# Opening of a two-layer decoder trunk: first conditioning vectors summed by the vector engine from smaller loads, the second in a PSUM bank of its own, unread products between one-column products

## The chip, the cores and the metric

The kernel runs on one core of a Trainium2 chip. The time is device microseconds of one execution of the whole program; several runs give a median. One further execution is profiled, and all rows below come from it.

## The reference

Two layers. Each layer has a mixer (latent attention with 4 heads beside a gated short convolution) and a channel mixer (dense SwiGLU in layer 0, top-2 of 8 SwiGLU experts in layer 1). x has 256 tokens of 1024 values. All of it is conditioned by six vectors of 1024 values per layer:

```
c_act = jax.nn.silu(c)
for l in range(DEPTH):
    mod = (c_act @ w_ada[l] + b_ada[l])[:, None, :]
    shift1, scale1, gate1, shift2, scale2, gate2 = jnp.split(mod, 6, axis=-1)
    h = x * (1 + scale1) + shift1
    y = hybrid_mixer(h, ...)                  # begins with z = h @ w_in
    x = layer_norm(DEEPNORM_ALPHA * x + gate1 * y, ln1_g[l], ln1_b[l])
    h = x * (1 + scale2) + shift2
    ...
```

w_ada is 1024 x 6144 per layer, so each vector costs 4 MB of weights and a product with a single row. Nothing in the kernel can begin before shift1 and scale1 of layer 0.

## The kernel before

All weights come through a ring of 7 slots of 2 MB (`raw`), filled by SyncE (SP) in the order of the list `loads`; before it fills a slot again, SP waits for a semaphore that says that the slot's old content is used. The list begins with four strips of w_ada (half a vector's weights each: strips 0 and 1 make vector 0, the shift; strips 2 and 3 vector 1, the scale), then x, then `wa`, `wb`, `wc` (parts of w_in), then further strips between the parts of the mixer's weights. Strips below `EARLY` come in two halves, with a semaphore for each.

A vector is formed so. A strip lies in its slot as four chunks of 128 rows and 1024 columns. The vector engine (DVE, `ada_part`, L950) multiplies a chunk by a column of c_act and adds it to `ada_acc`, whose start value the scalar engine (ACT, `ada_init`, L559) writes from the bias. TensorE (PE) then sums `ada_acc` over its 128 rows by eight one-column products against `ones` (L1543), which also turn the vector into 8 columns. For strips 1, 2 and 3 (`PE_ROWS`) PE takes the last chunk itself, by eight one-column products with c_act (L1539). Both vectors go through PSUM bank 7; the list `BANK7` gives the order of its uses, with the transpose of the small parameters (L1580) between the two, and ACT empties the bank after each (`drain_ada`, L570).

PE runs its own queue in order. Ahead of the products of each of the two vectors stand products of 512 columns that go to bank 4 and that nobody reads (L1576, L1583): they keep PE at work. After the second vector PE transposes x (L1570, 16 transposes); ACT and DVE write h_t from it (L587, L968); and L1607 multiplies h_t by wa, 16 products of 448 columns in 12 us. Behind it come the units of the mixer (L1590 to L1592), each a third of a product in split precision. A product of fp32 operands leaves two records in the trace, a transpose one.

Of the kernel before, what the change touches and what calls it, by code (L numbers as in the profile page):

```python
# [79 lines left out]
BANK7 = [("ada", 0, 0, 0), "params", ("ada", 0, 1, 0)]  # L80
PE_ROWS = (1, 2, 3)
# [8 lines left out]
EARLY = 4  # L90
# [27 lines left out]
def trunk(nc, a, out):  # L118
    with ExitStack() as ctx:
# [5 lines left out]
        def sem(name):  # L125
# [155 lines left out]
        half_full = [sem(f"half_full{k}") for k in range(EARLY)]  # L281
# [4 lines left out]
        prm_loaded, x_loaded, ln_loaded, rt_loaded = (sem("prm_loaded"), sem("x_loaded"), sem("ln_loaded"),  # L286
                                                      sem("rt_loaded"))
# [53 lines left out]
        def load_ada(l, n):  # L341
            k = ADA_ORDER.index(("ada", l, n))
            src, parts = strip_src(l, n), 2 if k < EARLY else 1
            loads.append((("ada", l, n), [(q * SLOT // parts, (q + 1) * SLOT // parts, 4 // parts,
                                           src[:, q * 4 // parts:(q + 1) * 4 // parts, :]) for q in range(parts)],
                          (bank7_full, BANK7.index(("ada", l, n // 2, 0)) + 1) if k < EARLY else (ada_summed, k + 1)))

# [5 lines left out]
        for l in range(L):  # L353
            z0 = ZA
            load_pe(("wa", l), [(0, KC * ZA, KC, win_src(l, 0, ZA))], (za_mm, TT * (l + 1)))
# [34 lines left out]
        for n, (name, parts, _) in enumerate(loads):  # L390
            filled[n % RING] += 16 * (1 if n < EARLY else len(parts))
            place_of[name] = n % RING
            full_at[name] = filled[n % RING]
        L0 = len(loads)

# [54 lines left out]
        def _(sp):  # L450
            sp.dma_start(c_col[:, :], a["c"].rearrange("a (k p) -> p (a k)", p=P),
                         allow_slow_non_contiguous=True).then_inc(c_loaded, 16)
            for n, (name, parts, _) in enumerate(loads):
                if n >= RING:
                    s, value = loads[n - RING][2]
                    sp.wait_ge(s, value)
                for lo, hi, chunks, src in parts:
                    dst = raw[n % RING][:, lo:hi].rearrange("p (c n) -> p c n", c=chunks)
                    sp.dma_start(dst, src).then_inc(half_full[n] if n < EARLY and lo == 0 else slot_full[n % RING], 16)
                if name == ("ada", 0, 3):  # L460
                    for t in range(TT):
                        sp.dma_start(x_sb[:, t, :], a["x"][0, t * P:(t + 1) * P, :]).then_inc(x_loaded, 16)
# [82 lines left out]
        def _(act):  # L545
# [30 lines left out]
            def modulate(v, l, row, last, t):  # L576

                if v == 0:
                    act.wait_ge(bank7_free, bank7(last) + 1)
# [37 lines left out]
            act.wait_ge(consts, 1)  # L617
            drain_ada(0, 0)
            act.wait_ge(bank7_full, bank7("params") + 1)
            act.activation(prm[:, :], ps[:, 7, 0:PRM], ACT.Copy).then_inc(bank7_free, 1)  # L620
            drain_ada(0, 1)

            def mixer(l):
                if l == 0:
                    modulate(0, 0, 0, ("ada", 0, 1, 0), 0)
                    modulate(0, 0, 0, ("ada", 0, 1, 0), 1)
# [28 lines left out]
                unit(2)  # L655
                for t in range(TT):
# [265 lines left out]
        def _(dve):  # L922
# [8 lines left out]
            def ada_part(l, n, first, last):  # L931
# [4 lines left out]
                for c in range(first, last):  # L936
                    if c == 0:
                        if k < EARLY:
                            dve.wait_ge(half_full[k], 16)
                        else:  # L940
                            wait_load(dve, name)
                        if kh == 0:
                            dve.wait_ge(ada_set, k // 2 + 1)
                        else:
                            dve.wait_ge(ada_summed, k)
                    if c == 2 and k < EARLY:
                        wait_load(dve, name)
                    if c == 3 and k in PE_ROWS:
# [10 lines left out]
            def modulate(v, l, row, last, t):  # L959
                if v == 0:  # L960
                    dve.wait_ge(bank7_free, bank7(last) + 1)
# [38 lines left out]
            dve.wait_ge(consts, 1)  # L1000
            dve.wait_ge(c_ready, 1)
            for n in range(4):
                ada(0, n)

# [41 lines left out]
            def mixer(l, behind):  # L1046
                if l == 0:
                    modulate(0, 0, 0, ("ada", 0, 1, 0), 0)
                    modulate(0, 0, 0, ("ada", 0, 1, 0), 1)
# [152 lines left out]
            dve.wait_ge(x_loaded, 16 * TT)  # L1202
# [318 lines left out]
        def _(pe):  # L1521
# [4 lines left out]

            def ada(l, vec, part=0):
# [4 lines left out]
                if 2 * k < EARLY:  # L1532
                    pe.wait_ge(c_ready, 1)
                    rows = [n for n in (2 * vec, 2 * vec + 1) if n in PE_ROWS]
                    for n in rows:
                        wait_load(pe, ("ada", l, n))
                        w = slot_of(("ada", l, n))[:, 3 * D:4 * D]
                        for c in range(KC):
                            pe.matmul(ps[:, 7, c:c + 1], w[:, c * P:(c + 1) * P], c_act[:, 4 * (n % 2) + 3:4 * (n % 2) + 4],  # L1539
                                      start=(n == rows[0] and c == 0), stop=False, skip_group_check=True)  # L1540
                    pe.wait_ge(ada_summed, 2 * (k + 1))
                    for c in range(KC):
                        m = pe.matmul(ps[:, 7, c:c + 1], acc[:, c * P:(c + 1) * P], ones[:, 0:1],  # L1543
                                      start=False, stop=True, skip_group_check=True)
                    m.then_inc(bank7_full, 1)
                    return
# [14 lines left out]
            def turn_input(v, t):  # L1561
# [4 lines left out]
                else:  # L1566
                    pe.wait_ge(x_loaded, 16 * TT)
# [26 lines left out]
            def mixer(l):  # L1594
# [4 lines left out]
                wait_load(pe, ("wa", l))  # L1599
                wa = slot_of(("wa", l))[:, 0:KC * ZA].rearrange("p (c n) -> p c n", c=KC)  # L1600
                order = ((0, 4, 1, 5, 2, 6, 3, 7), range(KC))[l]
                for t in range(TT):
                    for n, c in enumerate(order):
# [403 lines left out]
```

## Time and profile before

| | |
|---|---|
| three runs | 1488.74, 1495.96, 1496.12 us; median 1495.96 |
| profiled execution, its own time | 1490.59 us |
| its span, first to last instruction | 1488.8 us |
| mean granted TensorE clock | 0.984 of 2.4 GHz |
| PE busy | 1430.2 us, 96% |
| DVE busy | 1262.4 us, 85% |
| ACT busy | 1000.1 us, 67% |

Times in rows are counted from the start of the span. A busy PE is not PE at its peak: its work is pipelined, and the ends of its records are modelled, so what a product costs is read from start to start. The granted clock is printed as a part of 2.4 GHz; its two levels are 1.00 and 0.50.

### The profile page before, as it was taken

What the parts mean: (1) busy time and instruction counts of PE and PEld (TensorE: products, weight loads), DVE (VectorE), ACT (ScalarE), POOL (GpSimd) and SP (SyncE); (2) the same over time, 40 slices, a digit from 0 to 9 for tenths busy, and PEclk for the clock granted to TensorE, in tenths of its full rate; (3) what the DMA queues carried; (4) which work ended last, traced back from release to release, by engine and by line L of the source; (5) the groups of instructions that cost most, each with busy time, mean ns of one, the idle gap of its engine ahead of it and who ended that gap; (6) DMA issues with size and microseconds to landing.
All of it is one profiled execution on the core that took longest, in us unless ns stands there. A gap on an engine that the chain in (4) does not pass through costs nothing.

```text
span 1488.8 us, 20198 instructions
## 1 busy us (share of the span) xinstructions
PE 1430.2 (96%) x7131; PEld 1169.6 (79%) x7131; DVE 1262.4 (85%) x1432; ACT 1000.1 (67%) x1188; POOL 19.8 (1%) x60
## 2 busy tenths in 40 slices
PE   7999999999999999999999999999999999999994
PEld 5875899996955788788788878878878877887883
DVE  5796887776768898898898989889889889889997
ACT  2523444354333788888888888888888888887883
POOL 1000000000000000000000000000000000001000
PEclk8999999999998999999999999999999999999998
DMA  9993678876572599999999999999999999999960
GB/s 363 395 403 143 224 289 326 298 269 253 215 297 89 217 390 356 364 386 355 368 372 365 365 362 391 359 362 375 362 367 372 361 368 371 374 358 378 410 252 30
DMA packets 203457, 482.18 MB, mean 324 GB/s; under 512 B 6928, under 2 KB 31614, under 8 KB 203402
## 3 DMA queue, kind: packets, MB, share of 16 engines
q1 hardware_dynamic: 198832, 470.31, 84.2%
q0 software_dynamic: 1584, 5.77, 1.0%
q10 hardware_dynamic: 2986, 5.38, 1.0%
q8 instruction: 33, 0.54, 0.1%
q14 instruction: 22, 0.18, 0.0%
HBM read 475.67 MB, written 5.77 MB: 323 GB/s over the span
## 4 chain that ended last, share of the span: by engine, by line
PE 84%; DVE 7%; ACT 6%; issue 3%; DMA 1%; ACTq 0%; DVEq 0%; SPq 0%
PE ps L1590 24%; PE ps L1592 23%; PE ps L1591 23%; ACT w_hi L809 2%; PE ps L1751 2%; PE ps L1928 2%; DVE low L1257 2%; PE ps L1607 2%; DVE ada_acc L950 1%; ACT h_t L840 1%; PE ps L1708 1%; PE ps L1552 1%; DMA raw<-in_w_ada_dram 1%; PE ps L1570 1%; ACT L809 1%
## 5 line engine op out<-in xcount | busy, mean ns | idle before, releaser
L1257 DVE TENSOR_TENSOR low<-raw,w_hi 128x1024 fp32r<-128x1024 f32 x672 | 790.3, 1220 | 67.7 <-ACT w_hi L809 53.1
L809 ACT ACTIVATE w_hi<-raw 128x1024 fp32r<-128x1024 f32 x672 | 701.3, 1062 | 132.2 <-PE ps L1592 127.8
L1590 PE MATMUL ps<-w_hi,h_lo 128*128 128x512 f32 x896 | 356.6, 398 | 10.3 <-DVE low L1257 9.8
L1592 PE MATMUL ps<-w_hi,h_hi 128*128 128x512 f32 x896 | 349.8, 390 | 0.0
L1591 PE MATMUL ps<-low,h_hi 128*128 128x512 f32 x896 | 349.1, 390 | 0.0
L1590 PE MATMUL ps<-w_hi,hid_lo 128*128 128x512 f32 x536 | 211.4, 394 | 7.4 <-DVE low L1257 4.9
L1590 PEld LDWEIGHTS ps<-w_hi,h_lo 128*128 128x128 f32 x896 | 168.2, 188 | 54.0 <-DVE low L1257 19.7
L1591 PE MATMUL ps<-low,hid_hi 128*128 128x512 f32 x536 | 208.8, 390 | 0.0
L1592 PE MATMUL ps<-w_hi,hid_hi 128*128 128x512 f32 x536 | 208.8, 390 | 0.0
L1592 PEld LDWEIGHTS ps<-w_hi,h_hi 128*128 128x128 f32 x896 | 168.2, 188 | 36.3
L1591 PEld LDWEIGHTS ps<-low,h_hi 128*128 128x128 f32 x896 | 168.5, 188 | 33.1
L950 DVE SCALAR_TENSOR_TENSOR ada_acc<-raw,c_act,ada_acc 128x1024 f32<-128x1024 f32 x93 | 119.0, 1281 | 11.2 <-ACT ada_acc L559 8.3
L1590 PEld LDWEIGHTS ps<-w_hi,hid_lo 128*128 128x128 f32 x536 | 100.7, 188 | 33.5 <-DVE low L1257 8.2
L1592 PEld LDWEIGHTS ps<-w_hi,hid_hi 128*128 128x128 f32 x536 | 100.6, 188 | 21.2
L1591 PEld LDWEIGHTS ps<-low,hid_hi 128*128 128x128 f32 x536 | 100.7, 188 | 19.8
L1590 PE MATMUL ps<-h_hi,low 128*128 128x256 f32 x320 | 92.6, 289 | 1.0 <-ACT sil L746 1.0
L1591 PE MATMUL ps<-h_lo,w_hi 128*128 128x256 f32 x320 | 90.5, 283 | 0.0
L1592 PE MATMUL ps<-h_hi,w_hi 128*128 128x256 f32 x320 | 90.5, 283 | 0.0
L1186 DVE TENSOR_TENSOR low<-raw,w_hi 128x1024 fp32r<-128x1024 f32 x62 | 74.9, 1222 | 13.5 <-ACT w_hi L760 12.6
L1192 DVE TENSOR_TENSOR h_t<-ps,sil 128x512 f32<-128x512 f32 x67 | 46.2, 690 | 42.1 <-ACT sil L746 24.2
L760 ACT ACTIVATE w_hi<-raw 128x1024 fp32r<-128x1024 f32 x62 | 63.6, 1053 | 26.3 <-PE ps L1592 25.9
L1590 PEld LDWEIGHTS ps<-h_hi,low 128*128 128x128 f32 x320 | 61.3, 191 | 2.5 <-ACT sil L746 1.2
(335 smaller groups left out, 1423.2 us busy)
## 6 DMA issues: line engine op xcount, KB each, us to landing
raw<-in_moe_w_gate_dram SPq DMA_DIRECT2D x56, 2048.0 KB, 9.3
raw<-in_moe_w_up_dram SPq DMA_DIRECT2D x56, 2048.0 KB, 9.6
raw<-in_moe_w_down_dram SPq DMA_DIRECT2D x56, 2048.0 KB, 9.2
raw<-in_w_ada_dram SPq DMA_DIRECT2D x20, 2048.0 KB, 9.0
raw<-in_w_in_dram SPq DMA_DIRECT2D x6, 2048.0 KB, 16.0
raw<-in_ffn_w_gate_dram SPq DMA_DIRECT2D x11, 1024.0 KB, 8.2
raw<-in_ffn_w_up_dram SPq DMA_DIRECT2D x11, 1024.0 KB, 10.5
raw<-in_ffn_w_down_dram SPq DMA_DIRECT2D x11, 1024.0 KB, 9.5
```

The source lines that it names most:

```text
L760: act.activation(w_hi[:, u % SRING, :], slot_of(name)[:, lo:lo + UNIT], ACT.Copy).then_inc(unit_hi, 1)
L809: act.activation(w_hi[:, (FF_UNITS + k) % SRING, :], raw[moe_slot(m)][:, (k % 4) * UNIT:(k % 4 + 1) * UNIT], ACT.Copy).then_inc(unit_hi, 1)
L950: ins = dve.scalar_tensor_tensor(acc, w[:, c, :], c_act[:, 4 * kh + c:4 * kh + c + 1], acc, ALU.mult, ALU.add)
L1186: dve.tensor_tensor(low_of(name)[:, lo:lo + UNIT], slot_of(name)[:, lo:lo + UNIT], w_hi[:, u % SRING, :].bitcast(F32), ALU.subtract).then_ ...
L1192: dve.tensor_tensor(hid, ps[:, 1, :].rearrange("p (f n) -> p f n", f=4), sil[:, :].rearrange("p (f n) -> p f n", f=4), ALU.mult).then_inc( ...
L1257: dve.tensor_tensor(low[moe_slot(m)][:, part], raw[moe_slot(m)][:, part], w_hi[:, q, :].bitcast(F32), ALU.subtract).then_inc(unit_lo, 1)
L1590: pe.matmul(o, x_lo, hi, start=first, stop=False, skip_group_check=True)
L1591: pe.matmul(o, x_hi, lo, start=False, stop=False, skip_group_check=True)
L1592: return pe.matmul(o, x_hi, hi, start=False, stop=last, skip_group_check=True)
L1607: m = pe.matmul(ps[:, 4 + t, 0:ZA], h_t[:, c, t * P:(t + 1) * P], wa[:, c, :], start=(n == 0), stop=(n == KC - 1))
L1751: m = pe.matmul(ps[:, (0, 5)[t] + half, :], a_t[:, c, t * P:(t + 1) * P], oa[:, c, half * 512:(half + 1) * 512], start=(c == 0), stop=(c = ...
L1928: m = pe.transpose(ps[:, 2, f * P:(f + 1) * P], hid[:, f, :], ident[:, :])
```

## The change

- Strips 0 to 3 come in 4, 2, 2 and 4 parts (`EARLY_PARTS`), and wa of layer 0 in two.
- DVE takes all chunks of strips 0, 1 and 3; of strip 2 PE takes two (`PE_CHUNKS`) and DVE two. The first chunk of a vector is a plain multiplication into `ada_acc`, with no start value; the last chunk of strip 3 is added in two halves.
- The bias of both vectors comes from PE: 16 one-column products of the 12 bias rows with a column of the identity (`early_bias`). Vector 1 is summed in bank 6, with semaphores `scale_full` and `scale_ready`.
- Ahead of the first sum stand 12 unread products of 512 columns instead of 5; the 3 ahead of the second vector are gone, and one stands behind each pair of one-column products with strip 2, 8 in all.
- The transpose of the parameters and their copy, and the start value of vector 3, move behind the transposes of x and behind ACT's first three `w_mix`.
- PE and DVE wait for the two halves of x apart, and L1607 takes the chunks in the order 0 to 7 (before: 0, 4, 1, 5, 2, 6, 3, 7).

```
-BANK7 = [("ada", 0, 0, 0), "params", ("ada", 0, 1, 0)]
-PE_ROWS = (1, 2, 3)
+BANK7 = [("ada", 0, 0, 0), "params"]
-EARLY = 4
+EARLY_PARTS = (4, 2, 2, 4)
+EARLY = len(EARLY_PARTS)
+PE_CHUNKS = (2, 3)
...
             def ada_init(k):
 
-                if k >= 2:
+                if k == 3:
+                    act.wait_ge(scale_full, 1)
+                elif k >= 2:
...
+            def drain_scale():
+                act.wait_ge(scale_full, 1)
+                act.activation(modc[:, 0, 1, :], ps[:, 6, 0:KC], ACT.Identity, bias=ones[:, 0:1]).then_inc(scale_ready, 1)
...
-            act.wait_ge(ident_ready, 1)
-            act.wait_ge(bias_loaded, 16)
-            ada_init(0)
-            ada_init(1)
...
+            act.wait_ge(bias_loaded, 16)
             drain_ada(0, 0)
-            act.wait_ge(bank7_full, bank7("params") + 1)
-            act.activation(prm[:, :], ps[:, 7, 0:PRM], ACT.Copy).then_inc(bank7_free, 1)
-            drain_ada(0, 1)
+            drain_scale()
...
                 unit(2)
+                if l == 0:
+                    act.wait_ge(bank7_full, bank7("params") + 1)
+                    act.activation(prm[:, :], ps[:, 7, 0:PRM], ACT.Copy).then_inc(bank7_free, 1)
+                    ada_init(3)
...
+                    if k == 2 and c in PE_CHUNKS:
                         continue
-                    ins = dve.scalar_tensor_tensor(acc, w[:, c, :], c_act[:, 4 * kh + c:4 * kh + c + 1], acc, ALU.mult, ALU.add)
-                    if c < (2 if k in PE_ROWS else 3):
+                    col = c_act[:, 4 * kh + c:4 * kh + c + 1]
+                    if k < EARLY and kh == 0 and c == 0:
+                        link(dve.tensor_scalar(acc, w[:, c, :], col, None, ALU.mult))
+                        continue
+                    if k == EARLY - 1 and c == 3:
+                        dve.scalar_tensor_tensor(acc[:, 0:512], w[:, c, 0:512], col, acc[:, 0:512], ALU.mult, ALU.add).then_inc(ada_half, 1)
+                        dve.scalar_tensor_tensor(acc[:, 512:], w[:, c, 512:], col, acc[:, 512:], ALU.mult, ALU.add).then_inc(ada_summed, 1)
+                        continue
...
+            def early_bias(k, bank):
+
+                for c in range(KC):
+                    pe.matmul(ps[:, bank, c:c + 1], ada_bias[0:L * VECS, c * P:(c + 1) * P], ident[0:L * VECS, k:k + 1],
+                              start=(c == 0), stop=False, skip_group_check=True)
+
+            def early_sum(k, bank, chunks):
+
+                for c in chunks:
+                    m = pe.matmul(ps[:, bank, c:c + 1], ada_acc[:, k, c * P:(c + 1) * P], ones[:, 0:1],
+                                  start=False, stop=True, skip_group_check=True)
+                return m
+
+            def warm_load(n, times):
+
+                wait_load(pe, ("ada", 0, n))
+                for _ in range(times):
+                    pe.matmul(ps[:, 4, :], ident[:, :], slot_of(("ada", 0, n))[:, 0:512], start=True, stop=True)
...
             pe.wait_ge(ident_ready, 1)
-            wait_load(pe, ("ada", 0, 0))
-            for _ in range(5):
-                pe.matmul(ps[:, 4, :], ident[:, :], slot_of(("ada", 0, 0))[:, 0:512], start=True, stop=True)
-            ada(0, 0)
+            pe.wait_ge(bias_loaded, 16)
+            early_bias(0, 7)
+            early_bias(1, 6)
+            warm_load(0, 12)
+            pe.wait_ge(ada_summed, 2)
+            early_sum(0, 7, range(KC)).then_inc(bank7_full, 1)
+            wait_load(pe, ("ada", 0, 2))
+            w = slot_of(("ada", 0, 2)).rearrange("p (c n) -> p c n", c=4)
+            for c in range(KC):
+                for q in PE_CHUNKS:
+                    pe.matmul(ps[:, 6, c:c + 1], w[:, q, c * P:(c + 1) * P], c_act[:, q:q + 1],
+                              start=False, stop=False, skip_group_check=True)
+                pe.matmul(ps[:, 4, :], ident[:, :], w[:, 0, 0:512], start=True, stop=True)
+            pe.wait_ge(ada_half, 1)
+            early_sum(1, 6, range(KC // 2))
+            pe.wait_ge(ada_summed, 4)
+            early_sum(1, 6, range(KC // 2, KC)).then_inc(scale_full, 1)
+            turn_input(0, 0)
+            turn_input(0, 1)
             use_bank7("params")
             pe.wait_ge(prm_loaded, 16 * PRM_LOADS)
             pe.transpose(ps[:, 7, 0:PRM], prm_rows[:, :], ident[0:PRM, 0:PRM]).then_inc(bank7_full, 1)
-            wait_load(pe, ("ada", 0, 2))
-            for _ in range(3):
-                pe.matmul(ps[:, 4, :], ident[:, :], slot_of(("ada", 0, 2))[:, 0:512], start=True, stop=True)
-            ada(0, 1)
-            turn_input(0, 0)
-            turn_input(0, 1)
```

Two places show how the instructions move. The first is PE from its first product to the products with wa; an arrow points from the operands to the output, `raw` is a slot, `x16` counts products that are alike. Before:

```order
L1576 MATMUL ps<-raw,ident 128x512 x5
L1539 MATMUL ps<-c_act,raw 128x1 x8
L1543 MATMUL ps<-ones,ada_acc 128x1 x8
L1580 MATMUL ps<-ident,prm_rows 128x110
L1583 MATMUL ps<-raw,ident 128x512 x3
L1539 MATMUL ps<-c_act,raw 128x1 x16
L1543 MATMUL ps<-ones,ada_acc 128x1 x8
L1570 MATMUL ps<-ident,x_sb 128x128 x16
L1607 MATMUL ps<-raw,h_t 128x448 x16
```

The same stretch of PE in the changed kernel; of the eight pairs with their unread product the first two stand here:

```order
L1558 MATMUL ps<-ident,ada_bias 128x1 x16
L1572 MATMUL ps<-raw,ident 128x512 x12
L1564 MATMUL ps<-ones,ada_acc 128x1 x8
L1616 MATMUL ps<-c_act,raw 128x1 x2
L1618 MATMUL ps<-raw,ident 128x512
L1616 MATMUL ps<-c_act,raw 128x1 x2
L1618 MATMUL ps<-raw,ident 128x512
...
L1564 MATMUL ps<-ones,ada_acc 128x1 x8
L1602 MATMUL ps<-ident,x_sb 128x128 x16
L1627 MATMUL ps<-ident,prm_rows 128x110
L1652 MATMUL ps<-raw,h_t 128x448 x16
```

Ahead of the products with wa stood 8 unread and 40 one-column products; now there are 20 and 48, and the transpose of the parameters has moved behind those of x.

The second place is ACT from the first activation to the squares of the mixer (`gb_t,ssq`). Before, without the ten small loads between:

```order
L607 ACTIVATE c_act<-c_col 128x8
L559 ACTIVATE ada_acc<-ada_bias,ident 128x1024 x2
...
L570 ACTIVATE modc<-ps,eps 128x8
L559 ACTIVATE ada_acc<-ada_bias,ident 128x1024
L620 ACTIVATE prm<-ps 128x110
L570 ACTIVATE modc<-ps,ones 128x8
L559 ACTIVATE ada_acc<-ada_bias,ident 128x1024
L587 ACTIVATE h_t<-ps,modc 128x128 x8
...
L639 ACTIVATE w_mix<-raw 128x1024
L658 ACTIVATE gb_t,ssq<-ps 128x256
```

The same stretch of ACT in the changed kernel:

```order
L624 ACTIVATE c_act<-c_col 128x8
...
L587 ACTIVATE modc<-ps,eps 128x8
L572 ACTIVATE ada_acc<-ada_bias,ident 128x1024
L576 ACTIVATE modc<-ps,ones 128x8
L604 ACTIVATE h_t<-ps,modc 128x128 x8
...
L651 ACTIVATE w_mix<-raw 128x1024
L670 ACTIVATE prm<-ps 128x110
L572 ACTIVATE ada_acc<-ada_bias,ident 128x1024
L674 ACTIVATE gb_t,ssq<-ps 128x256
```

The start values of vectors 0 and 1 are gone; the copy of prm and the start value of vector 3 have moved from ahead of h_t to ahead of the squares.

## Rows read from the trace of the kernel before

**Rows 1.** The page, part 4: the chain that ended last, by engine.

```profile
PE 84%; DVE 7%; ACT 6%; issue 3%; DMA 1%; ACTq 0%; DVEq 0%; SPq 0%
```

**Rows 2.** Timeline of PE, 0 to 48 us: start, us, engine, line, operation, records, idle before.

```profile
10.31 6.86 PE L1576 MATMUL ps<-raw,ident 128*128 128x512 f32 x10 [10.31 <-DMA raw<-in_w_ada_dram]
17.01 1.84 PE L1539 MATMUL ps<-c_act,raw 128*128 128x1 f32 x16
18.71 1.93 PE L1543 MATMUL ps<-ones,ada_acc 128*128 128x1 f32 x16
21.20 4.45 PE L1583 MATMUL ps<-raw,ident 128*128 128x512 f32 x6
25.49 3.93 PE L1539 MATMUL ps<-c_act,raw 128*128 128x1 f32 x32
29.29 3.55 PE L1543 MATMUL ps<-ones,ada_acc 128*128 128x1 f32 x16
32.70 3.29 PE L1570 MATMUL ps<-ident,x_sb 128*128 128x128 f32 x16
35.83 12.19 PE L1607 MATMUL ps<-raw,h_t 128*128 128x448 f32 x32
```

**Rows 3.** Timeline of DVE, two pieces of its sums.

```profile
9.21 13.11 DVE L950 SCALAR_TENSOR_TENSOR ada_acc<-raw,c_act,ada_acc 128x1024 f32<-128x1024 f32 x10 [8.25 <-ACT ada_acc L559]
...
26.31 1.28 DVE L950 SCALAR_TENSOR_TENSOR ada_acc<-raw,c_act,ada_acc 128x1024 f32<-128x1024 f32 x1 [0.22 <-DMA raw<-in_w_ada_dram]
```

**Rows 4.** PE by stretches: length, busy (records), granted clock, DMA share, GB/s.

```profile
10.30:15.00 4.70, 4.69 (x6) 1.00 1.02 394
15.00:17.00 2.00, 2.00 (x5) 1.00 1.05 413
21.90:25.20 3.30, 3.30 (x5) 0.50 1.05 409
25.30:28.60 3.30, 3.30 (x30) 1.00 1.02 409
28.70:35.40 6.70, 6.70 (x33) 0.50 1.05 404
35.60:40.00 4.40, 4.40 (x16) 1.00 1.05 409
```

**Rows 5.** The chain in order of time, a run of transposes at the upper level.

```profile
144.91 0.87 PE ps L1570 x8
```

**Rows 6.** Timeline of SP's queue, issues behind x: start, time to issue.

```profile
14.28 10.73 SPq L459 DMA_DIRECT2D raw<-in_w_in_dram  x2
29.68 5.69 SPq L459 DMA_DIRECT2D raw<-in_w_ada_dram  x1
```

**Rows 7.** Timeline of ACT.

```profile
7.92 1.15 ACT L559 ACTIVATE ada_acc<-ada_bias,ident 128x1024 f32<-128x1024 f32 x1 [3.35 <-DMA ada_bias<-in_b_ada_dram]
...
32.88 0.27 ACT L570 ACTIVATE modc<-ps,ones 128x8 f32<-128x8 f32 x1 [10.69 <-PE ps L1543]
...
48.06 0.38 ACT L658 ACTIVATE gb_t<-ps 128x256 f32<-128x256 f32 x1 [4.53 <-PE ps L1607]
```

**Rows 8.** Groups of DVE by form: busy us, mean ns, idle before.

```profile
L996 DVE TENSOR_SCALAR yv<-yv,meanvar,rstd 128x1024 f32<-128x1024 f32 x6 | 4.9, 812 | 0.2
```

**Rows 9.** DMA issues up to 75 us: size, median us from issue to landing.

```profile
raw<-in_w_in_dram SPq DMA_DIRECT2D x1, 1792.0 KB, 19.5
```

**Rows 10.** Groups of weight loads by form.

```profile
L1539 PEld LDWEIGHTS ps<-c_act,raw 128*128 128x128 f32 x48 | 6.1, 203 | 1.3 <-issue 1.3
...
L1853 PEld LDWEIGHTS ps<-router_b,ones 1*128 1x128 f32 x4 | 0.6, 182 | 0.0
```

**Rows 11.** All engines by stretches; the last two numbers are DMA share and GB/s.

```profile
50.00:75.00 25.00, 25.00 (x212) 25.00 (x211) 19.45 (x27) 11.76 (x17) 0.00 (x0) 1.00 0.97 385
...
100.00:110.00 10.00, 10.00 (x46) 7.18 (x46) 9.72 (x14) 2.60 (x3) 0.00 (x0) 0.98 1.06 404
```

**Rows 12.** Waits from 35 us to the end that a DMA ended: total us, times, longest.

```profile
ACT w_mix L639 <- DMA raw<-in_w_in_dram: 0.6, 1, 0.6
```

More of the change, by code:

```diff
@@ L280, in trunk @@
         slot_full = [sem(f"slot_full{k}") for k in range(RING)]
-        half_full = [sem(f"half_full{k}") for k in range(EARLY)]
+        part_full = [[sem(f"part_full{k}_{q}") for q in range(parts - 1)] for k, parts in enumerate(EARLY_PARTS)]
+        wa_half, ada_half = sem("wa_half"), sem("ada_half")
+        scale_full, scale_ready = sem("scale_full"), sem("scale_ready")
         ada_set, ada_summed = sem("ada_set"), sem("ada_summed")
@@ L354, in trunk @@
             z0 = ZA
-            load_pe(("wa", l), [(0, KC * ZA, KC, win_src(l, 0, ZA))], (za_mm, TT * (l + 1)))
+            halves = 2 if l == 0 else 1
+            load_pe(("wa", l), [(q * KC * ZA // halves, (q + 1) * KC * ZA // halves, KC // halves,
+                                 win_src(l, 0, ZA)[:, q * KC // halves:(q + 1) * KC // halves, :]) for q in range(halves)],
+                    (za_mm, TT * (l + 1)))
             load_pe(("wb", l), [(0, SLOT, KC, win_src(l, z0, z0 + D_CONV))], (mix_used, MIX_UNITS * l + 4))
@@ L390, in trunk @@
         for n, (name, parts, _) in enumerate(loads):
-            filled[n % RING] += 16 * (1 if n < EARLY else len(parts))
+            filled[n % RING] += 16 * (1 if n < EARLY or name == ("wa", 0) else len(parts))
             place_of[name] = n % RING
@@ L394, in trunk, with part_sem @@
         L0 = len(loads)
+        def part_sem(n, name, q, parts):
+            if q < parts - 1 and n < EARLY:
+                return part_full[n][q]
+            return wa_half if name == ("wa", 0) and q == 0 else slot_full[n % RING]
         def slot_of(name):
@@ L456, in _ @@
                     sp.wait_ge(s, value)
-                for lo, hi, chunks, src in parts:
+                for q, (lo, hi, chunks, src) in enumerate(parts):
                     dst = raw[n % RING][:, lo:hi].rearrange("p (c n) -> p c n", c=chunks)
-                    sp.dma_start(dst, src).then_inc(half_full[n] if n < EARLY and lo == 0 else slot_full[n % RING], 16)
+                    sp.dma_start(dst, src).then_inc(part_sem(n, name, q, len(parts)), 16)
                 if name == ("ada", 0, 3):
                     for t in range(TT):
-                        sp.dma_start(x_sb[:, t, :], a["x"][0, t * P:(t + 1) * P, :]).then_inc(x_loaded, 16)
+                        sp.dma_start(x_sb[:, t, :], a["x"][0, t * P:(t + 1) * P, :]).then_inc(x_loaded[t], 16)
             def expert_loads(i, e, first, store):
@@ L937, in ada_part @@
                     if c == 0:
[L938 to L939 removed]
+                        if k >= EARLY:
+                            wait_load(dve, name)
+                        if kh == 1:
+                            dve.wait_ge(ada_summed, k)
+                        elif k >= EARLY:
+                            dve.wait_ge(ada_set, k // 2 - 1)
+                    if k < EARLY and c % (4 // EARLY_PARTS[k]) == 0:
+                        q = c * EARLY_PARTS[k] // 4
+                        if q < EARLY_PARTS[k] - 1:
+                            dve.wait_ge(part_full[k][q], 16)
                         else:
                             wait_load(dve, name)
[L942 to L948, printed above, removed]
[L949 to L951 removed]
+                    if k == 2 and c in PE_CHUNKS:
+                        continue
+                    col = c_act[:, 4 * kh + c:4 * kh + c + 1]
[6 more added lines that the diff above has]
+                        continue
+                    ins = dve.scalar_tensor_tensor(acc, w[:, c, :], col, acc, ALU.mult, ALU.add)
+                    if c < (min(PE_CHUNKS) - 1 if k == 2 else 3):
                         link(ins)
@@ L1200, in hidden_lo @@
                                   ALU.subtract).then_inc(hid_lo_ready, 1)
-            dve.wait_ge(x_loaded, 16 * TT)
+            for t in range(TT):
+                dve.wait_ge(x_loaded[t], 16)
             mixer(0, lambda t: None)
@@ L1531, in ada @@
                 acc = ada_acc[:, k % 2, :]
[L1532 to L1546, printed above, removed]
                 pe.wait_ge(ada_summed, 2 * (k + 1))
@@ L1597, in mixer @@
                     turn_input(2, 0)
-                wait_load(pe, ("wa", l))
+                if l == 0:
+                    pe.wait_ge(wa_half, 16)
+                else:
+                    wait_load(pe, ("wa", l))
                 wa = slot_of(("wa", l))[:, 0:KC * ZA].rearrange("p (c n) -> p c n", c=KC)
-                order = ((0, 4, 1, 5, 2, 6, 3, 7), range(KC))[l]
                 for t in range(TT):
-                    for n, c in enumerate(order):
+                    for n, c in enumerate(range(KC)):
+                        if l == 0 and t == 0 and n == KC // 2:
+                            wait_load(pe, ("wa", l))
                         if l == 1 and t == 0 and n == 6:
```

25 lines of the change are left out of this document (13 added, 12 removed).

## The prediction

> **What bounds the kernel now.** I read the page first. PE is busy for 96% of the span, and the chain that ended last is 84% PE [rows 1], so time in the opening counts only where PE is what is waited for. Then I took the timeline of PE up to its first large product, L1607 [rows 2]. The reader is to see one idle stretch, up to 10.31 us, when the first strip of w_ada is there, and behind it work almost without a gap until L1607 starts at 35.83. That work is 8 products of 512 columns that nobody reads (16 records, since one fp32 product leaves two), 40 one-column products (80 records: 16, 16, 32 and 16) and 17 transposes. So PE's own queue bounds the opening, not the vector engine and not the loads: DVE's last product of the second vector starts at 26.31 and takes 1.28 [rows 3], it is over at 27.6, and PE comes to the sum that reads it only at 29.29 [rows 2]. Last I took the granted clock by stretches [rows 4]: 0.50 (1.2 GHz) from 21.9 to 25.2 and from 28.7 to 35.4, 1.00 (2.4 GHz) between. Both falls come behind stretches in which PE ran little but one-column products. At the very start the column says 1.00, but there 6 records lie in 4.70 us and right after 5 in 2.00, so the first 4.7 us of work ran at the lower level too.
>
> **Prices.** A 512-column record costs 0.43 us at the upper level and 0.85 at the lower (10 records from 10.31 to 17.01: 4.7/0.85 + 2.0/0.43 = 10.2). A one-column record costs 0.106 to 0.12 at the upper level (16 in 1.70, 32 in 3.80, start to start), I take 0.115, and 0.213 at the lower (16 from 29.29 to 32.70) [rows 2, 4]. A transpose at the upper level is 0.87/8 = 0.109 [rows 5]; the 16 of the opening took 3.13, at the lower.
>
> **Loads.** The same bytes come in the same order. The diff adds five issues on SP's queue (4+2+2+4 in place of 8 for w_ada, 2 in place of 1 for wa); they lie beside transfers that hold SP anyway (5.69 us for one issue at 29.68 [rows 6]). The last part of strip 3 therefore lands at 26.3 as now. The smaller first parts let DVE start near 6 us in place of 9.21, where it waits for ACT's start value [rows 3, 7], but then it follows the loads: its end is 26.3 plus two halves of 0.67, 27.6, the same as now. I cost this at nothing. The first product as tensor_scalar, 0.81 us by the nearest row [rows 8] against 1.28, twice, lies ahead of a wait for a load: nothing too. wa in halves saves nothing: the whole of it lands at 14.28 + 19.5 = 33.8 [rows 6, 9], before L1607 starts.
>
> **PE, step by step.** PE's queue is in order, so each item delays all behind it.
> 1. Bias products: 16 of one column, 32 records, as soon as ada_bias is there, 7.92 by ACT's row [rows 7]. PE is cold, so 32 x 0.213 = 6.8 us, to 14.75. The bounds are 32 x 0.115 = 3.7 and 6.8; I take the upper, because the first products of the kernel now run at the lower level and no rise has come behind one-column products [rows 2, 4]. That they have 12 rows changes little: the load of a weight of one row takes 182 ns, of 128 rows 203 in the mean of both levels [rows 10].
> 2. Unread products: 12, so 24 records, 24 x 0.427 = 10.25 at the upper level, plus half of the time spent at the lower. That time is now 4.7 us at the start and 3.4 from 21.8; I take 3.6 (bounds 2.5 and 4.7): 12.1, to 26.85. Strip 0 is there at 10.3 and DVE's first vector at about 18.4 (7 products from 9.21 now), so neither ends this step.
> 3. The sum of the first vector, 16 records: 1.85, to 28.7. ACT's drain behind it is not late for anything; it also frees slots 0 and 1, to which SP comes at 29.68 [rows 6].
> 4. The third strip: eight times two one-column products and one of 512 columns, 8 x (4 x 0.115 + 2 x 0.427) = 10.5, to 39.2.
> 5. The sum of the second vector, which DVE has had ready since 27.6: 1.85, to 41.05.
> 6. 16 transposes: 1.75 at the upper level, to 42.8, and the one of the parameters, 0.1. ACT writes the scale in 0.27 [rows 7] and its first h_t beside them.
>
> L1607 starts at 42.9 in place of 35.83: **+7.0 us**. The same by difference: 12 more unread products, +10.25; eight more one-column products, +1.8; an earlier start, -2.25; idle gaps gone, -0.5; less time at the lower level, -2.3.
>
> What else moves has cover. The copy of prm (some 0.3) and the start value of vector 3 (1.15) now stand on ACT behind w_mix, ahead of the squares of L658; ACT waits 4.53 us for PE there [rows 7], and without that cover they would cost 1.4. SP waits for scale_full at 41.05, where it waited for bank 7 until 32.8; queued behind are strips and wu. It has issued 19.7 MB by then (four strips, x, wa, wb, wc, two strips) and about 15.5 have moved at 0.41 MB/us [rows 11], so the DMA engines have work for 10 us more.
>
> **Does it pass on?** From 35 us to the end the waits name a DMA as releaser once, for 0.6 us (ACT, for wb) [rows 12], where ACT has L1607's 12 us as cover. Slots are freed by PE and DVE, which move by the same 7 us. So I pass the shift on in full: span 1488.8 + 7.0 = 1495.8. The profiled execution's own time is 1490.59, which makes 1497.6. It was one of the faster: the three runs have a median of 1495.96, and the four executions lie in two pairs, near 1489.7 and 1496.0. I add 2.4, which brings the own time to their mean of 1493, and give **1500 us**, 0.3 to 0.5% over before, by which of these one counts.
>
> **A rule against the rows.** The rows show a rise of the clock at 35.5, behind 16 transposes at the lower level, and L1607 runs high from there [rows 2, 4]. The Trainium skill, TensorE: Matmul & The Clock Gate, Part 4 (PE-mode transpose), says of transposes that they do not count as PE-busy in the same way and that the full clock does not engage for them. The trace does not agree. By the rows L1607 starts high, 1500; by the Trainium skill the sums and transposes would leave the clock low and L1607 would begin there, which is the second half of rival E.
>
> **Rivals.**
> - B: PE starts at the upper level. For it: the granted column reads 1.00 from the first record. Against: the pace of the records [rows 4]. Step 1 is then 3.7 and step 2 10.25: L1607 at 37.9, +2.1, 1495.
> - C: the delay is absorbed. The DMA engines are full until 110 us [rows 11]; if the stages behind L1607 really follow the loads, a later PE finds them further on and catches up: +0, 1493. It decides if PE's units wait for landings now. Against: [rows 12].
> - D: faster. The unread products run only where PE would wait for DVE. DVE done at 27.6, the second half of the sum 0.9, transposes 1.75, h_t 0.4: L1607 between 31 and 34 (wa at 33.8), -2 to -4.5, about 1490. It needs PE at the second sum by 26.9, so steps 1 to 4 in 19 us; the rows give 31.
> - E: the clock falls within the opening. If step 4, two thirds of it 512-column work, has one low stretch of 3.4 us: +1.7. If the last sum, the transposes and the start of L1607 run low: 1.6 + 1.4 + 1.7 = 4.7. With the 7.0 that is +8.7 to +11.7, 1502 to 1505. For it: one-column records stood ahead of the fall at 28.7. Against: step 4 is dense, and the transposes went with a rise [rows 2, 4].
>
> **Chances.** Forecast 0.57, B 0.10, C 0.10, D 0.08, E 0.15. About 0.5% (7.5 us) is what a measurement of this kernel can tell from no change, and the forecast lies just inside it. D never reaches that: faster 0.02. Slower: E and two fifths of the forecast, 0.38. Within: 0.60. The range goes from C less 2 to E's upper end plus 2, 1491 to 1507; D lies outside.
>
> **What would show it.** In the timeline of PE: bias products from 8 us for about 7; 24 unread records until 26 to 28; the block of c_act and unread products for 10 to 11 us; the second sum after 39, with DVE idle for over 10 us before its h_t; L1607 at about 43. Step 1 is wrong if the bias products take under 4 us, step 2 if its pace is 0.43 from the first record. The passing on is wrong if a DMA appears as a releaser behind 50 us, or if the stages from L1607's start to the end are not the 1488.8 - 35.8 = 1453 us of now.

## The result

Thirteen runs of each kernel: 1493.16 us before (1488.74 to 1496.19), 1498.49 us changed (1496.49 to 1501.17). The ratio of changed to before is 1.0041, 95% interval 1.0029 to 1.0053: slower by about 6 us, clear of noise, and under the 0.5% that the prediction named. The forecast was 1500 us, in a range of 1491 to 1507, with +7.0 us for the change.

The timeline of PE in the changed kernel, from its first product to the product with wa, now on line L1652 (columns as in [rows 2]). Of the eight pairs of one-column products and their unread product (L1616, L1618) the first three and the last stand here.

```profile
6.34 6.95 PE L1558 MATMUL ps<-ident,ada_bias 12*128 12x1 f32 x32 [6.34 <-DMA ada_bias<-in_b_ada_dram]
13.22 13.34 PE L1572 MATMUL ps<-raw,ident 128*128 128x512 f32 x24
26.39 1.84 PE L1564 MATMUL ps<-ones,ada_acc 128*128 128x1 f32 x16
28.10 0.58 PE L1616 MATMUL ps<-c_act,raw 128*128 128x1 f32 x4
28.54 1.55 PE L1618 MATMUL ps<-raw,ident 128*128 128x512 f32 x2
29.88 0.85 PE L1616 MATMUL ps<-c_act,raw 128*128 128x1 f32 x4
30.60 2.03 PE L1618 MATMUL ps<-raw,ident 128*128 128x512 f32 x2
32.44 0.53 PE L1616 MATMUL ps<-c_act,raw 128*128 128x1 f32 x4
...
39.36 1.10 PE L1618 MATMUL ps<-raw,ident 128*128 128x512 f32 x2
40.30 1.84 PE L1564 MATMUL ps<-ones,ada_acc 128*128 128x1 f32 x16
42.00 1.95 PE L1602 MATMUL ps<-ident,x_sb 128*128 128x128 f32 x16
43.78 0.26 PE L1627 MATMUL ps<-ident,prm_rows 110*128 110x110 f32 x1
43.88 12.21 PE L1652 MATMUL ps<-raw,h_t 128*128 128x448 f32 x32
```

The reader is to see that no row behind the first has a wait, and that the product with wa starts at 43.88 us where it started at 35.83 [rows 2]. DVE shows the other side: it has done the second vector at 27.8 and then waits 15.45 us for PE's transposes. Its timeline:

```profile
5.93 0.75 DVE L970 TENSOR_SCALAR ada_acc<-raw,c_act 128x1024 f32<-128x1024 f32 x1 [4.98 <-DMA raw<-in_w_ada_dram]
...
27.02 0.75 DVE L974 SCALAR_TENSOR_TENSOR ada_acc<-raw,c_act,ada_acc 128x512 f32<-128x512 f32 x1
43.21 2.64 DVE L995 TENSOR_SCALAR h_t<-ps,modc 128x128 f32<-128x128 f32 x8 [15.45 <-PE ps L1602]
```

The granted clock in stretches, to be set against [rows 4]: two levels again, the lower one only from 29.2 to 32.5 as the column has it. The first 5.7 us of L1572, from 13.22 to 18.90, ran at the lower level too, though the column reads 1.00: the 9 records of that row are 7 of L1572 and the last 2 of one column, and 7 records in 5.68 us is the lower level's pace.

```profile
13.00:18.90 5.90, 5.90 (x9) 1.00 1.03 391
19.00:26.30 7.30, 7.30 (x18) 1.00 1.03 415
...
29.20:32.50 3.30, 3.30 (x10) 0.50 1.05 404
32.60:41.00 8.40, 8.40 (x45) 1.00 1.05 409
```

The stages behind did not catch up. In the profiled executions the time from the start of the product with wa to the end of the span was 1488.8 - 35.8 = 1453.0 us and is 1499.0 - 43.9 = 1455.1. No wait behind 35 us was ended by a DMA. From 50 to 100 us the DMA share is now 0.83, where it was 1.00 in the same stretch of before: the slots are freed later, and the DMA engines wait for PE (SP waits 10.9 us for the product with wa before it fills a slot again, where it waited 2.1).

```profile
50.00:100.00 50.00, 50.00 (x351) 1.00 0.83 328
```

The profiled execution of before, with its own time of 1490.59, is one of the faster, and that of the changed kernel, 1500.84, one of the slower. The 10 us between them are therefore more than the change costs.

### The profile page after: what moved, and what is told of

It is laid out like the page before. It is cut to its first block, busy times and chain, and to the rows that moved or that the text cites. A ratio compares the mean times of both kernels' runs of the same rounds, so it can differ in the third digit from the quotient of the medians.

```text
span 1499.0 us, 20284 instructions
## 1 busy us (share of the span) xinstructions
PE 1442.3 (96%) x7171; PEld 1175.7 (78%) x7171; DVE 1263.2 (84%) x1434; ACT 998.0 (67%) x1186; POOL 19.7 (1%) x60
## 4 chain that ended last, share of the span: by engine, by line
PE 84%; DVE 7%; ACT 6%; issue 3%; DMA 0%; ACTq 0%; DVEq 0%; POOL 0%; POOLq 0%
PE ps L1631 23%; PE ps L1633 23%; PE ps L1632 23%; ACT w_hi L825 2%; PE ps L1753 2%; DVE low L1285 2%; PE ps L1973 2%; PE ps L1652 2%; ACT h_t L856 1%; PE ps L1796 1%; PE ps L1572 1%; DVE ada_acc L976 1%; PE ps L1584 1%; PE ps L1618 1%; ACT L825 1%
## 5 line engine op out<-in xcount | busy, mean ns | idle before, releaser
L1631 PEld LDWEIGHTS ps<-w_hi,hid_lo 128*128 128x128 f32 x536 | 100.7, 188 | 33.5 <-DVE low L1285 8.1
```

Of the source, the lines that this page charges most:

```text
L1631: pe.matmul(o, x_lo, hi, start=first, stop=False, skip_group_check=True)
```

## The experiments

Eleven kernels. My theory: PE's queue, in order and without gaps, sets when the product with wa starts, and everything behind moves with it. The rivals: the delay is absorbed by stages that follow the loads; the unread products pay for themselves through the clock; other parts of the change cost or bring the time. Except where it is said, each kernel is an edit of the changed one. Ratios are to the kernel before, with 95% intervals.

**Fewer unread products ahead of the first sum.**

```
-            warm_load(0, 12)
+            warm_load(0, 5)
```

> The changed kernel with 5 unread products ahead of the first sum instead of 12. Theory (PE's own queue sets when the product with wa starts): 14 records fewer, at the upper level 6.0 us, up to 7.5 with the lower; the product with wa starts between 36.4 and 38.1 us instead of 43.88, and the time falls by 6 to 7.5 us from the changed kernel's 1498.5, to about 1492, the time of before. Rival (absorption: the stages behind follow the loads): no change, 1498.5. Rival (the unread products pay for themselves through the clock): falls of the clock cost 3 us or more of it back, 1494 to 1496.

Measured: 1491.72 us (12 runs), ratio 0.9995 (0.9985 to 1.0005), the same as before. Its timeline of PE:

```profile
13.10 6.62 PE L1572 MATMUL ps<-raw,ident 128*128 128x512 f32 x10
19.55 1.84 PE L1564 MATMUL ps<-ones,ada_acc 128*128 128x1 f32 x16
...
31.78 1.84 PE L1564 MATMUL ps<-ones,ada_acc 128*128 128x1 f32 x16
...
35.36 12.21 PE L1652 MATMUL ps<-raw,h_t 128*128 128x448 f32 x32
```

The block ends at 19.55 in place of 26.39, and the clock did not fall in the third strip's block in this execution, so the product with wa is 8.5 us earlier, a microsecond below the expected range. In the median the time fell by 6.8 us. The seven unread products carry the whole net loss: what else the change adds to PE's queue and takes from it comes out even (35.36 against 35.83 in [rows 2]). Neither absorption nor a clock that needs them holds.

**No unread products between the one-column products.**

```
-                pe.matmul(ps[:, 4, :], ident[:, :], w[:, 0, 0:512], start=True, stop=True)
```

> The changed kernel without the 8 unread products between the one-column products of strip 2. Theory: 16 records fewer, 6.8 us at the upper level; the one-column products, sum and transposes may run at the lower level for one or two stretches and give 2 to 4 us back: the product with wa starts between 36 and 41 us, the time is 1491 to 1495. Rival (the clock is what matters): the clock falls through the whole of it and 5 us or more are given back, 1497 or more. Absorption: 1498.5.

Measured: 1497.58 us, ratio 1.0025 (1.0009 to 1.0041). The runs lie in groups, five at 1491.8 to 1492.9, three at 1497.5 to 1498.0 and four at 1500.5 to 1501.0. In the profiled one, of the last group, the lower level lasts from 29.3 to 42.9 us. The columns are those of [rows 4]:

```profile
19.10:29.20 10.10, 10.10 (x42) 1.00 1.03 412
29.30:42.90 13.60, 13.60 (x62) 0.50 1.05 408
```

The product with wa starts at 41.35, 2.5 us before the changed kernel's, so of the 6.8 us that the queue gives 4.3 went to the clock in this one. The clock rival holds at least in this execution, and by the groups in a part of the runs; the 1491 to 1495 of the theory is missed by the median.

**Both.** The two edits together.

> Both together: 5 unread products ahead of the first sum, none between. Theory: PE now reaches the second sum at 26 to 29 us, close to where the vector engine ends its last half (27.7), and the product with wa starts at 33 to 36 us, 8 to 10 us before the changed kernel; 1489 to 1491, 2 to 4 us under the kernel before. Clock rival: the sums and transposes run low, start at 36 to 38, 1492 to 1494. Absorption: 1498.5.

Measured: 1490.19 us, ratio 0.9993 (0.9980 to 1.0005). PE now waits for DVE, for the first time in the opening, 1.23 us ahead of the second sum. Its timeline:

```profile
22.08 4.07 PE L1616 MATMUL ps<-c_act,raw 128*128 128x1 f32 x32
27.37 3.58 PE L1564 MATMUL ps<-ones,ada_acc 128*128 128x1 f32 x16 [1.23 <-DVE ada_acc L973]
30.81 3.65 PE L1602 MATMUL ps<-ident,x_sb 128*128 128x128 f32 x16
34.26 0.39 PE L1626 MATMUL ps<-ident,prm_rows 110*128 110x110 f32 x1
34.44 12.74 PE L1651 MATMUL ps<-raw,h_t 128*128 128x448 f32 x32
```

Sum and transposes run at the lower level (3.44 and 3.45 us start to start, against 1.70 and 1.78 in the changed kernel). The start at 34.44 is within what was expected, the gain in time over before is not measurable. The runs lie in two groups here too, eight at 1488.8 to 1490.6 and four at 1493.4 to 1494.1; the profiled one is of the lower.

**The loads cut as before.**

```
-EARLY_PARTS = (4, 2, 2, 4)
+EARLY_PARTS = (2, 2, 2, 2)
...
-            halves = 2 if l == 0 else 1
+            halves = 1
```

> The changed kernel with the loads cut as before: strips 0 to 3 in two halves each, wa in one piece. Theory: PE's queue sets the start of the product with wa, so the parts are worth nothing through the vector engine; only if they made the bias land earlier (6.34 us against 7.92) does PE begin 1.6 us later. So 0 to +1.6 us, the product with wa at 43.9 to 45.5. A rival in which the smaller first loads help the vector engine on the path would give +3 us (DVE starts at 9 to 10 instead of 5.9).

Measured: 1499.31 us (6 runs), ratio 1.0060 (1.0038 to 1.0083), not told apart from the changed kernel's 1.0041. PE and DVE both start later. PE's timeline:

```profile
8.47 6.96 PE L1558 MATMUL ps<-ident,ada_bias 12*128 12x1 f32 x32 [8.47 <-DMA ada_bias<-in_b_ada_dram]
...
43.77 12.21 PE L1649 MATMUL ps<-raw,h_t 128*128 128x448 f32 x32
```

And the first row of DVE's sums, from its timeline:

```profile
8.22 0.75 DVE L970 TENSOR_SCALAR ada_acc<-raw,c_act 128x1024 f32<-128x1024 f32 x1 [7.27 <-DMA raw<-in_w_ada_dram]
```

PE starts 2.1 us later and still comes to the product with wa 0.1 us earlier, just under the expected 43.9 to 45.5. In this pair of traces the later start is made up for: here the clock did not fall in the third strip's block (10.5 us against 12.2), there it did, and the unread block is 0.6 us shorter. Six runs, two of them at 1503.3 and 1507.2, can't tell whether the earlier bias is worth its 2 us. That DVE starts 2.3 us later is seen nowhere on the path.

**12 unread products in the kernel before.** One part of the change alone: 5 becomes 12 in the loop on L1576 of the kernel before.

> The kernel before with one part of the change alone: 12 unread products ahead of the first sum instead of 5. Theory: 14 records at the upper level, 6.0 us, all on PE's path: L1607 starts at 41 to 43 us, time 4.5 to 7.5 us over the kernel before. Absorption: no difference. A rival in which the rest of the change is what costs: no difference here either.

Measured: 1497.74 us (6 runs), ratio 1.0042 (1.0026 to 1.0057), the same as the whole change. L1607 starts 5.3 us later than in [rows 2], and the rest takes 1494.2 - 41.2 = 1453.0 us, as before.

```profile
10.44 12.06 PE L1576 MATMUL ps<-raw,ident 128*128 128x512 f32 x24 [10.44 <-DMA raw<-in_w_ada_dram]
...
41.16 12.19 PE L1607 MATMUL ps<-raw,h_t 128*128 128x448 f32 x32
```

**Few unread products: 4 and 4.**

```
-            warm_load(0, 12)
+            warm_load(0, 4)
...
-                pe.matmul(ps[:, 4, :], ident[:, :], w[:, 0, 0:512], start=True, stop=True)
+                if c % 2:
+                    pe.matmul(ps[:, 4, :], ident[:, :], w[:, 0, 0:512], start=True, stop=True)
```

> The changed kernel with 4 unread products ahead of the first sum and 4, not 8, between the one-column products. Theory (PE's queue, and the clock kept up by a few unread products): bias products to 13.3, unread to 19.3, first sum to 21, third strip 3.7 + 3.4 = 7.1 us to 28.2, where the vector engine has just ended (27.7); sum and transposes at the upper level, 3.6 us: the product with wa starts at 32 us, 3.8 us before the kernel before, 12 before the changed one. Time 3 to 4 us under the kernel before. Rival (the clock falls anyway in sums and transposes): start at 34 to 36, no difference from before. Absorption: no difference either, but then with a start at 32 in the trace.

Measured: 1496.09 us, ratio 1.0011 (0.9991 to 1.0031). Two groups of runs: four at 1486.4 to 1489.5, eight at 1495.6 to 1500.7. The profiled one is of the upper group. Its granted clock, in a stretch as in [rows 4]:

```profile
23.40:40.40 17.00, 17.00 (x59) 0.50 1.04 409
```

PE's timeline in that stretch and behind it:

```profile
25.04 1.70 PE L1616 MATMUL ps<-c_act,raw 128*128 128x1 f32 x8
26.61 2.05 PE L1619 MATMUL ps<-raw,ident 128*128 128x512 f32 x2
...
38.77 13.04 PE L1653 MATMUL ps<-raw,h_t 128*128 128x448 f32 x32
```

The lower level holds for 17 us, and the product with wa starts at 38.8, not 32. The expectation failed for two runs in three; in the profiled one it was the clock, for the other seven that is inferred from their group. Two runs of the lower group, 1486.4 and 1486.7, are shorter than any run of the kernels up to here, and that group's times fit a start near 32; no trace shows one of them. With 4 unread products ahead PE also came too early for strip 2 and waited 0.45 us for its load at 20.2 us, just before the fall at 23.4. The next kernel has no such wait, and its clock falls as well.

**Few, with 10 unread products ahead of the bias products.** 8 unread ahead of the first sum, 4 between, and from 2.3 us ten products of the identity with itself.

> As the kernel with few unread products, and 10 unread products of 128 columns (identity by identity) from 2.3 us, ahead of the bias products; 8 unread products ahead of the first sum. Theory: the bias products run at the upper level, 3.7 us in place of 6.95, if the clock has risen by 6.3 us; the 8 unread ones then end near 18 to 20 us and the product with wa starts at 32, as with few: the gain at the bias products is not on the path. Rival (step 1's 7 us are on the path at any count of unread products): start 3 us earlier than with few.

Measured: 1498.13 us, ratio 1.0016 (0.9992 to 1.0039), again two groups (1486.7 to 1492.9 and 1497.9 to 1501.4). The timeline of PE from its first product:

```profile
2.29 4.56 PE L1606 MATMUL ps<-ident 128*128 128x128 f32 x20 [2.29 <-POOL ident L524]
6.77 4.03 PE L1558 MATMUL ps<-ident,ada_bias 12*128 12x1 f32 x32
10.73 10.16 PE L1572 MATMUL ps<-raw,ident 128*128 128x512 f32 x16
```

The bias products take 3.96 us start to start in place of 6.88, which is the price that the prediction had as its lower bound, 3.7. But the clock was down again from 10.0 to 16.7 us and from 23.6 to about 44, PE reached the first sum at 20.7 with 8 unread products, and the product with wa started at 41.98, not 32. The test of whether the bias products' 7 us are on the path is spoilt by the falls; it stays open from this run.

**Do transposes bring the clock up?** The kernel called "both", with 48 more transposes ahead of the 16.

> The kernel with 5 unread products ahead of the first sum and none between, plus 48 more transposes of x into bank 4, unread, ahead of the 16 that are needed. It asks whether transposes bring the clock up. If they do: they start at the lower level near 31 us, 0.21 us apart, rise within 3 to 7 us to 0.11 apart, and end after 7 to 9 us; the product with wa starts at 42 to 44. If they don't (the rule of the Trainium skill): all 64 at 0.21, 13.6 us, the product with wa at 48 and itself low at first.

One run, 1497.09 us. Its granted clock by stretches while PE ran the 48 and the 16:

```profile
30.50:36.20 5.70, 5.70 (x29) 0.53 1.05 408
36.30:40.20 3.90, 3.90 (x38) 1.00 1.05 408
```

PE's timeline there:

```profile
30.48 8.07 PE L1624 MATMUL ps<-ident,x_sb 128*128 128x128 f32 x48
38.38 1.91 PE L1602 MATMUL ps<-ident,x_sb 128*128 128x128 f32 x16
...
40.23 12.21 PE L1654 MATMUL ps<-raw,h_t 128*128 128x448 f32 x32
```

They start at the lower level, 29 records in 5.70 us, of which the last 0.3 us, from 35.9, is already at the upper; from 36.3 it is 38 records in 3.90, with nothing but transposes on PE since 30.5. The product with wa starts at 40.2 and high. One execution, but a plain one: transposes of fp32 bring the clock up here. The range of 42 to 44 for the start was too late by 2 us.

**All of strip 2 on the vector engine.** The one-column products with c_act are gone, and the two conditions in DVE's `ada_part` that make it skip chunks 2 and 3 of strip 2. 5 unread products stand ahead of the first sum, 7 in one block behind it.

```
-            warm_load(0, 12)
+            warm_load(0, 5)
...
-            wait_load(pe, ("ada", 0, 2))
-            w = slot_of(("ada", 0, 2)).rearrange("p (c n) -> p c n", c=4)
-            for c in range(KC):
-                for q in PE_CHUNKS:
-                    pe.matmul(ps[:, 6, c:c + 1], w[:, q, c * P:(c + 1) * P], c_act[:, q:q + 1],
-                              start=False, stop=False, skip_group_check=True)
-                pe.matmul(ps[:, 4, :], ident[:, :], w[:, 0, 0:512], start=True, stop=True)
+            warm_load(2, 7)
```

> The changed kernel with all of strip 2 summed by the vector engine: PE has no one-column products with c_act (32 records gone), 5 unread products ahead of the first sum and 7 behind it in one block. Theory (PE's queue, with the clock kept up because the block is nothing but 512-column work): bias to 13.2, unread to 19.7, sum to 21.4, 7 unread to 27.4, the vector engine ends at 28.4, then 0.9 and 1.75 at the upper level: the product with wa starts at 31 to 32 us, 4 us before the kernel before, and in nearly every run, with no second group of runs 10 us later as with few unread products: 1487 to 1489, 3 to 5 us under before. Rival (DVE or the load of wa takes over): start at 33 to 34. Clock rival: two groups of runs, the median at or over before.

Measured: 1488.04 us (1486.89 to 1491.19, 12 runs), ratio 0.9975 (0.9964 to 0.9985). It has the lowest median here, it is faster than both kernels, and its runs lie in one group. PE's timeline from the block of seven:

```profile
21.94 6.25 PE L1570 MATMUL ps<-raw,ident 128*128 128x512 f32 x14
28.46 1.95 PE L1562 MATMUL ps<-ones,ada_acc 128*128 128x1 f32 x16 [0.27 <-DVE ada_acc L971]
30.27 2.39 PE L1600 MATMUL ps<-ident,x_sb 128*128 128x128 f32 x16
32.46 0.39 PE L1619 MATMUL ps<-ident,prm_rows 110*128 110x110 f32 x1
32.64 13.40 PE L1644 MATMUL ps<-raw,h_t 128*128 128x448 f32 x32
```

PE and DVE now meet within 0.3 us at the second sum. The start is 32.64, 3.2 us before [rows 2]; 0.6 later than expected, mostly because the clock fell at 31.7 in this execution. Two things changed at once, the one-column products gone and the unread ones in one block; no run tells them apart.

**Six between.** 5 ahead of the first sum, and the unread product left out behind every fourth pair.

> The changed kernel with 5 unread products ahead of the first sum and 6, not 8 and not 4, between the one-column products. With 8 the clock stayed up and the product with wa started at 35.4; with 4 it fell in most runs. Theory: if six are enough, start at 33.7 and 1.7 us under the kernel with 5 and 8, 1490; if not, the falls cost 5 to 8 us in a part of the runs and the median is 1494 to 1497, as with 4. The queue alone says 1490; where the line between 4 and 8 lies is open.

Measured: 1490.95 us (11 runs, 1488.6 to 1492.9), ratio 0.9995 (0.9986 to 1.0004). The start is at 33.42 and the level upper throughout; there is no second group. As a time, it is not told apart from before.

**The same as with all of strip 2 on the vector engine, wa in one piece.**

> As the kernel with all of strip 2 on the vector engine, but wa of layer 0 in one piece. In the prediction wa in halves was worth nothing, since PE came to it at 42.9, long after its landing. With PE there at 31.5 the halves should be worth what is missing until the whole lands (33 to 33.5): start at 33.4 against 31.5, +1.5 to +2 us. Rival: the whole lands before PE comes, no difference.

Measured: 1488.72 us, ratio 0.9978 (0.9966 to 0.9990), no difference from the kernel with halves. The expected 1.5 to 2 us did not come. PE does wait for wa, but only 0.72 us, as its timeline has it:

```profile
32.66 12.29 PE L1641 MATMUL ps<-raw,h_t 128*128 128x448 f32 x32 [0.72 <-DMA raw<-in_w_in_dram]
```

The whole of wa lands at 32.6, not at 33 to 33.5. wa in halves is worth 0.7 us at most, and only to a PE that comes this early.

## Why the prediction was right, and where its terms were off

**The place.** PE's queue sets the start of the product with wa: shown. Taking away seven unread products took the whole loss back, and putting seven into the kernel before gave the whole loss. DVE's earlier start changed nothing on the path. The smaller loads let PE start 2.1 us earlier; whether the time is shorter for it the runs can't tell.

**The steps**, predicted end and measured end in the trace of the changed kernel:

| step | forecast | measured |
|---|---|---|
| start of PE | 7.92 | 6.34 |
| 1 bias products | 6.8, to 14.75 | 6.88, to 13.22 |
| 2 unread products | 12.1, to 26.85 | 13.17, to 26.39 |
| 3 first sum | 1.85, to 28.7 | 1.71, to 28.10 |
| 4 third strip | 10.5, to 39.2 | 12.2, to 40.30 |
| 5 second sum | 1.85, to 41.05 | 1.70, to 42.00 |
| 6 transposes | 1.85, to 42.9 | 1.88, to 43.88 |

The start was 1.6 us too late, since I let ada_bias land when it landed before. Step 2 was 1.1 too short: the first lower stretch was 5.7 us, not 3.6. Step 4 was 1.7 too short in this execution, because the clock fell once in it, from 29.2 to 32.5. That is the first half of rival E, priced at 1.7. The kernel with 5 unread products ahead ran the same step without a fall, 10.5 us (21.25 to 31.78), so the term is right where the clock holds. The kernel with the loads as before did so too (29.66 to 40.18). How often it falls in the changed kernel I can't say: only the profiled execution has a trace. The runs lie at 1496.5 to 1496.8, 1497.9 to 1498.9 and 1500.2 to 1501.2; that this is one fall more or less is a guess that fits the sizes.

So the path was right, and the 42.9 is near 43.88 partly by luck: the late start made up for more than half of what steps 2 and 4 lacked. Without the fall in step 4 the start would have been 42.2, +6.3 us (an estimate, 43.88 less 1.7). Two readings were off without effect: the last 0.6 of the 3.80 us for 32 one-column records ran at the lower level [rows 4], so 0.12 is no price of the upper; and the earlier start in the sum by difference is 10.31 - 7.92 = 2.39, not 2.25.

**Passing on.** Start of the product with wa and the rest of the span, in the profiled execution of each kernel:

| kernel | start | rest |
|---|---|---|
| before | 35.83 | 1453.0 |
| changed | 43.88 | 1455.1 |
| 5 ahead | 35.36 | 1455.3 |
| none between | 41.35 | 1457.9 |
| both | 34.44 | 1454.0 |
| loads as before | 43.77 | 1453.1 |
| before with 12 | 41.16 | 1453.0 |
| 4 and 4 | 38.77 | 1457.6 |
| all of strip 2 on DVE | 32.64 | 1452.6 |
| six between | 33.42 | 1453.4 |
| 4 and 4, with 10 ahead of the bias | 41.98 | 1455.3 |
| both, 48 more transposes | 40.23 | 1455.2 |
| all of strip 2 on DVE, wa whole | 32.66 | 1455.7 |

The start varies by 11 us and the rest by 5, and the rest is not shorter where the start is late. So nothing is absorbed, and rival C is out: the DMA share did fall behind 50 us, but no DMA ended a wait. By the prediction's own sign the rest should have been 1453; it was 2.1 us more, within the spread of the kernels, and where those 2.1 us arose is open. The spread of the rest is one reason why single profiled executions are poor for comparing times here.

**The rivals.** B, a PE at the upper level from its first product, is out: 32 one-column records took 6.88 us. D, faster, did not come for this change; but its arithmetic (a start at 31 to 34, -2 to -4.5) is what the kernel with all of strip 2 on DVE reached, 32.64 and -0.25%. Of E the first half came in the profiled execution. The second half, low sums and transposes ahead of the product with wa, came in the traces with none between ("both" and "none between") and with 4 between ("4 and 4" and the one with 10 products ahead of the bias), not in those with 8 or 6.

**The rule of the Trainium skill** (TensorE: Matmul & The Clock Gate, Part 4, PE-mode transpose), that the full clock does not engage for transposes: the trace of before spoke against it, and the kernel with 48 more transposes does so directly for the fp32 transposes used here, with a rise at 35.9 us in a stretch of nothing else, in one execution.

**The size.** The step that gave 1500 rests on 1493 + 7.0. The thirteen runs of before have a median of 1493.16, so the base was right. That was partly luck: it took four executions for two pairs, and eight of the thirteen lie between the pairs, at 1491.0 to 1493.8. The time went up by 5.3 us in the medians and by 6.1 in the ratio, against 7.0. I had put the real change just under the line of 0.5%, and it lies there.

## What to carry to other kernels

An unread product that keeps TensorE's clock up is free only in a gap. Work out when the engine would otherwise have waited (here for DVE, until 27.7 us) and give the filler no more than that; here seven products on a queue without a gap cost all of the 6 us, and the kernel without them was as fast as before. Less is not enough by itself: without any filler between the thin products PE came to the second sum in time to wait for DVE, and the low clock took most of the gain. Thin one-column products mixed with little filler left the clock to chance; moving the thin ones to the vector engine, which had time, and putting one block of filler in their place was the fastest way tried.

## What the runs showed of the hardware

- Between 32 one-column records, 8 and 6 unread products of 512 columns (with 5 ahead) gave runs within 4.3 us of each other and no fall in the third strip's block; with 8 and 12 ahead the trace has one of 3.3 us. With 4 between, eight runs of twelve (4 ahead) and seven of twelve (8 ahead) lie 5 us and more above the others, and the ones profiled spent 17 and some 20 us at 1.2 GHz. With none the clock also fell, in the trace for 13.6 us.
- A small transfer on ACT's queue (ada_bias, 48 KB) ended PE's wait at 6.2 to 6.9 us in nine traces with SP's first loads of 512 KB, and at 8.47 with loads of 1 MB (7.92 on ACT in [rows 7]). In the kernel with loads of 1 MB and in the changed one it was issued at the same time, 1.94 us. That the size of SP's loads is the cause rests on this one pair of traces.
- The granted clock column reads 1.00 at PE's first records in every trace, while they run at half the pace (in the changed kernel 7 records of 512 columns from 13.22 to 18.90 us, then 18 in 7.30).
- One-column products with 12 rows cost what those with 128 rows cost: 0.215 us a record at the lower level, against 0.213 [rows 2].
